# A two-block transformer layer in fp32 on one core: a weight split paced, a gate bank copied earlier, a clamp moved, filler products placed ahead of a wait

## What is computed

```python
def hybrid_layer(h, ...):                       # first layer, cut
    u = rmsnorm(h, norm_pre)
    proj = u @ w_in
    z_ssd, xbc, dt_raw, z_att, q, k, v, f_raw, g_raw = jnp.split(proj, cuts, axis=-1)
    xbc = silu(causal_depthwise_conv(xbc, conv_w, conv_b))
    y = ssd_chunked(xs_p, dt_p, a, bm_p, cm_p)  # state-space part, 4 groups x 9 chunks
    y_ssd = gated_group_rmsnorm(y + d_skip * xs, z_ssd, ssd_norm)
    y_att = forgetting_attention(qh, kh, vh, logf) * silu(z_att)
    merged = g_ssd * (y_ssd @ w_proj_ssd) + g_att * (y_att @ w_proj_att)
    return h + rmsnorm(merged @ w_out, norm_post)

def second_block(x, p, ...):                    # second layer, cut
    dq, dk, dv, bq, bk, bv, z = jnp.split(rms_norm(x) @ w_in, IN_SPLIT_IDX, axis=-1)
    dq = rms_norm(dq); dk = rms_norm(dk)        # per head, 64 wide
    a = rms_norm(diff_attention(dq, dk, dv, lam, diff_slopes))
    b = dilated_attention(rms_norm(bq), rms_norm(bk), bv, dil_slopes)
    x = x + (concat([a, b]) * silu(z)) @ w_out
    return x + sigmoid(rms_norm(x) @ w_ple_gate) * (p @ w_ple_proj)
```

## Time and profile before

| | |
|---|---|
| median of 3 executions | 2833.82 us (2832.86 to 2835.63) |
| the profiled execution | 2834.69 us, of it 2832.9 us from first to last instruction |
| PE busy | 2738.8 us, 97% of the span |
| DVE, ACT, POOL busy | 60%, 37%, 33% |
| DMA | 236.55 MB, mean 84 GB/s |
| TensorE clock granted, mean | 0.991 of full speed |

### The profile page before, as it was taken

The page is one execution under the profiler, slowest core; times in us unless marked ns, Lnnn a source line. Parts: engine busy times, 40 slices in busy tenths (PEclk is TensorE's granted clock), DMA queues, the critical chain, the costliest instruction groups (busy, mean ns, idle before and its releaser), DMA issues. The chain is left out here.

```text
span 2832.9 us, 39662 instructions
## 1 busy us (share of the span) xinstructions
PE 2738.8 (97%) x15660; PEld 2126.4 (75%) x15660; DVE 1699.7 (60%) x2674; ACT 1043.4 (37%) x1727; POOL 928.2 (33%) x549
## 2 busy tenths in 40 slices
PE   7999999999999999999999999999999999999999
PEld 6979797987778777777776887766666667776777
DVE  5787878786121345444456114776776786677586
ACT  4342524343110233333333002335666654444231
POOL 2233323232554111111111334542221134333465
PEclk8999999999999999999999999999999999999999
DMA  4131413233533111111112324531101101113643
GB/s 170 60 88 67 88 69 85 72 79 111 209 112 116 46 53 44 52 40 44 53 46 108 106 80 143 178 100 41 48 19 44 38 24 52 42 42 99 221 142 108
DMA packets 113752, 236.55 MB, mean 84 GB/s; under 512 B 9120, under 2 KB 52896, under 8 KB 113568
## 3 DMA queue, kind: packets, MB, share of 16 engines
q1 hardware_dynamic: 63312, 172.14, 18.5%
q10 hardware_dynamic: 50256, 61.87, 7.3%
HBM read 189.88 MB, written 44.11 MB: 83 GB/s over the span
## 5 line engine op out<-in xcount | busy, mean ns | idle before, releaser
L80 PE MATMUL psum<-u_h,w_hi 128*128 128x512 f32 (+2 forms) x2624 | 1011.2, 385 | 27.0 <-ACT z_gate L622 9.7
L82 PE MATMUL psum<-u_h,w_lo 128*128 128x512 f32 (+2 forms) x2624 | 963.5, 367 | 0.0
L81 PE MATMUL psum<-u_h,w_hi 128*128 128x512 f32 (+2 forms) x2624 | 962.4, 367 | 0.0
L136 POOL TENSOR_SCALAR w_hi<-w_raw 128x1024 fp32r<-128x1024 f32 x212 | 236.1, 1114 | 1418.3 <-ACTq L1368 500.3
L80 PEld LDWEIGHTS psum<-u_h,w_hi 128*128 128x128 f32 x2624 | 495.8, 189 | 158.5 <-issue 73.6
L138 POOL TENSOR_TENSOR w_lo<-w_raw,w_hi 128x1024 fp32r<-128x1024 f32 x212 | 545.2, 2572 | 17.7
L81 PEld LDWEIGHTS psum<-u_h,w_hi 128*128 128x128 f32 x2624 | 496.3, 189 | 69.6 <-issue 11.5
L82 PEld LDWEIGHTS psum<-u_h,w_lo 128*128 128x128 f32 x2624 | 495.4, 189 | 68.8
L1393 ACT ACTIVATE f_exp<-psum 128x1024 f32<-128x1024 f32 (+5 forms) x104 | 78.8, 774 | 235.0 <-PE psum L1237 128.0
L2618 ACT ACTIVATE a_exp<-a_exp 128x1024 f32<-128x1024 f32 x96 | 101.4, 1056 | 119.9 <-DVE a_exp L2790 62.5
L1487 DVE CUSTOM_DVE_ANT_0 f_junk<-psum,f_decay,f_max 128x512 f32<-128x512 f32 (+2 forms) x96 | 60.2, 664 | 103.8 <-PE psum L1260 91.1
(11 more groups left out here) (433 smaller groups left out, 4445.4 us busy)
## 6 DMA issues: line engine op xcount, KB each, us to landing
w_raw<-in_w_all SPq DMA_DIRECT2D x212, 512.0 KB, 3.5
sums_rows<-s_acs ACTq DMA_DIRECT2D x32, 512.0 KB, 8.5
f_decay<-s_nc SPq DMA_DIRECT2D x16, 520.0 KB, 5.8
s_y<-conv_out ACTq DMA_DIRECT2D x16, 512.0 KB, 2.9
yo_raw<-s_y ACTq DMA_DIRECT2D x8, 1024.0 KB, 10.9
x_tok<-in_x SPq DMA_DIRECT2D x8, 512.0 KB, 8.4
s_xT<-xT SPq DMA_DIRECT2D x8, 512.0 KB, 4.9
s_pssd<-fox_last ACTq DMA_DIRECT2D x16, 256.0 KB, 2.0
```

What stands on the lines that cost most here:

```text
L80: nc.tensor.matmul(out, w_hi[:, k], a_hi, start=(k == 0 and first), stop=False)
L81: nc.tensor.matmul(out, w_hi[:, k], a_lo, start=False, stop=False)
L82: return nc.tensor.matmul(out, w_lo[:, k], a_hi, start=False, stop=(k == kk - 1 and final))
L136: self.nc.gpsimd.tensor_scalar(self.hi[:, r], self.raw[:, r], 1.0, 1.0, ALU.mult, ALU.mult).then_inc(self.hi_done, 1)
```

## The change

Five edits. In `lead_phase`, the first weight tile's split waits between its two steps for the fifth `spread` (`split` gets an argument for it), and eight filler products stand ahead of the last `spread_rows`. In `ssd_phase`, ACT copies the gate's second bank before the exponentials of chunk 1 instead of after, and DVE's `clamp(2)` stands behind the values and b of chunk 1 instead of ahead of `decay_c(1)`. In the second block, the filler products of the item `("S", 0, GK1)` stand ahead of the wait for the small bank instead of behind it, and are 12 instead of 8.

```diff
-    def split(self, eng, i, per, n):
+    def split(self, eng, i, per, n, between=None):
...
         eng.wait_ge(self.hi_done, m + 1)
+        if between is not None:
+            eng.wait_ge(*between)
         self.nc.gpsimd.tensor_tensor(self.lo[:, r], self.raw[:, r], self.hi[:, r].bitcast(F32),
...
+            hold(nc, K, ps[:, 512 * 7:512 * 7 + P], 8)
             spread_rows(NCH - 1)
             first_projection(1, 7, range(KT))
...
-            K.W.split(pool, 0, 0, 0)
+            K.W.split(pool, 0, 0, 0, (spread, 5))
...
-                for d in (1, 2):
-                    row_exps(d)
-                    exps(d)
-                    if d == 1:
-                        zcopies(1)
+                row_exps(1)
+                zcopies(1)
+                exps(1)
+                row_exps(2)
+                exps(2)
...
                 copy_b(0)
-                clamp(2)
                 decay_c(1)
...
+                        if c == 0:
+                            clamp(2)
                         mask(c + 1)
...
                 kind, q, g = it
+                if it == ("S", 0, GK1):
+                    hold(nc, K, ps[:, MX + 512:MX + 512 + P], 12)
                 least(pe, sfree, number[it])
...
-                    if (q, g) == (0, GK1):
-                        hold(nc, K, ps[:, MX + 512:MX + 512 + P], 8)
                     pe.wait_ge(sq_ok, number_of(q, g) + 1)
```

## The result

The changed kernel takes 2840.56 us in the median of 11 runs (2836.65 to 2843.45), the kernel before 2832.86 in 11 runs beside it (2830.59 to 2837.94). The ratio is 1.0028, with an interval of 1.0020 to 1.0036: **0.28% slower**, some 7.7 us, where the forecast was 5 us faster. The profiled execution has a span of 2841.0 us against 2832.9.

What follows compares the result with a forecast made beforehand. PE was taken as the bound, busy 2738.8 of 2832.9 us. Lead phase -3.1, state-space phase +1.7 and second block -3.7 sum to -5.1 us against 2834.69, so 2828.7 us on the median's scale, range 2825.0 to 2833.0.

Steps and rivals of the forecast that it cites:

- Part 2: State-space phase: group 0 gains, groups 1 to 3 and the clock lose; a loss of 1.7 us, ends -1.5 and +6.
- the turns go to POOL: Rival, state-space phase: groups 1 to 3 lose 1.8 us each, one more clock fall; phase +5.8, time 2832.8; chance 0.17.
- The sign that I had named: Groups 1 to 3: the fourth gate product would stand behind waits of 2.5 to 3 us.
- Group 0: State-space phase: values no longer wait behind the clamp; fourth gate product at 154.4 instead of 155.69, gain 1.3 us.
- Group 2: State-space phase: POOL had got in ahead of the mask there already, so a loss of only 0.1 us.
- The copy of the gate's bank: Groups 1 to 3: exponentials behind it bring the mask 0.9 us later; it wins a small wait that `front(2)` takes back.
- The clock: Ahead of the fourth gate product idle time grows; half a 1.7 us fall for group 3, less for group 0, 1.1 together.
- The lead phase: `x_diag` stall gone, fillers free and holding the clock, SP last; next phase at 45.2 instead of 48.34, gain 3.1 us.
- The second block: 24 filler passes run before the bank is free, 3.78 us at half clock vanish; gain 3.7 us, bounds 3.0 and 4.0.
- a little: Second block: chain to the first key product keeps 7.2 us, ending 1916.95; PE finishes its own products sooner and idles a little.
- The lower bound of 3.0: Second block: gain if fillers run at half clock, 5.8 us to 1910.8, where the chain starts with the sum.
- The slower case of the prediction: Rival: two idle ends of PE per group bring five new clock falls of 1.7 us; 2839.6 us, chance 0.05.

Runs made afterwards that it cites:

- clamp_before_b: Kernel before with only the clamp of chunk 2 moved, behind the values but ahead of the copy of b; 2833.16 us, ratio 1.0001.
- ssd_only: Kernel before with the two state-space edits alone (gate's second bank copied earlier, clamp of chunk 2 later); 2837.90 us, ratio 1.0017.
- clamp_only: Kernel before with only the clamp moved behind the values and the copy of b, in all four groups; 2837.33 us, ratio 1.0016.
- zcopy_only: Kernel before with only the copy of the gate's second bank moved ahead of the exponentials of chunk 1; 2838.02 us, ratio 1.0021.
- early4: Kernel before plus four short products of ones by ones (16 columns) at PE's very start; 2832.57 us, ratio 1.0000.
- early8: Kernel before plus eight products of ones by ones (128 columns) at PE's very start; 2834.61 us, ratio 1.0012.
- early16: Kernel before plus sixteen short products of ones by ones (16 columns) at PE's very start; 2834.96 us, ratio 1.0004.
- clamp_g0: Kernel before with the clamp moved in group 0 alone, the copy of the gate's bank left where it was; 2830.39 us, ratio 0.9996.
- all_again: The changed kernel with all edits, run again beside its parts, against the kernel before; 2837.21 us, ratio 1.0021.
- all_third: The changed kernel with all edits, run once more against the kernel before; 2837.94 us, ratio 1.0019.

## Why the prediction was wrong

**The turns at the clamp: the step that failed.** Part 2 let the moved clamp start at 292.88 and end at 294.02, since in the earlier trace rows it ran undisturbed against L400 with starts 0.04 us apart. The trace after has the same 0.04 us and the other winner: 2.09 us. The rule of the Trainium skill that I weighed there and set aside ("SBUF — State Buffer", section "Who interferes with whom": of the two, the one that issues first has the port pair for the whole instruction) was the right forecast, and clamp_before_b shows it at work: with a lead of 0.16 us DVE has the turn. Read with recorded starts it still gives the wrong winner for the pair of the earlier trace rows, as I had written; what failed was to carry that pair's outcome over to another pair with the same 0.04 us. The first rival, "the turns go to POOL", had the mechanism, its price (1.8 for each group, measured 1.6, 0.7 and 1.6) and a sum for the phase of +5.8; I gave it 0.17. The steps of the phase add up to -1.3 + 3.9 + 1.6 (clock) = +4.2 in ssd_only, where I had +1.7. From 48.3 to 700.5 the five executions with the whole edit come out 4.8 us later than the kernel before's, and five with none of it 0.4 earlier: +5.2. With the turn won (clamp_before_b) groups 1 and 3 lose 0.6 each, for which 0.9 was forecast. The sign that I had named, waits of 2.5 to 3 us ahead of the fourth gate products, came true (2.7) with the wrong step behind it.

**Group 0** was right: L491 waits for `cb` (1.67 us in the changed kernel) and the fourth gate product comes 1.36 us earlier, for 1.3 forecast.

**Group 2** was counted at 0.1, since POOL had got ahead there already. It lost 0.7 in ssd_only and clamp_only: the late mask adds to that state instead of taking its place. Behind the moved copy alone it does take its place (0.0 in zcopy_only).

**The copy of the gate's bank** was right in form: ACT brings the mask later too, and the later of the two counts. zcopy_only shows that this half alone loses 1.0 us in groups 1 and 3 and nothing in group 2, and 1.6 us more by a clock that stays down for longer. What it wins is the small wait ahead of the third gate product, and the chunk loop gives it back.

**The clock** behind the state-space groups was counted at 1.1 in all. The new fall behind group 3's fourth gate product comes in each of the seven executions that move the clamp there, at 1.6 to 1.7 us (clamp_before_b's too), and in none of the ten others (among all but those of early4, early8 and early16). That term was 0.5 too small.

**The lead phase: the chain was right, the fillers were not free.** `x_diag` at 20.70 with 0.29, the next phase at 45.03, SP the last to end: each as forecast, and the 3.1 us were 3.3 in this pair of executions. But the kernel before's own execution had a long fall of the clock in this phase. The clock in stretches of 3.41 us, in the kernel before and then in clamp_g0, which has the same lead phase:

```profile
22.97:26.38 3.41, 2.50 (x10) 2.10 (x10) 3.28 (x10) 1.00 (x2) 0.11 (x1) 0.51 0.01 2
26.38:29.79 3.41, 2.33 (x7) 2.06 (x8) 3.24 (x10) 3.14 (x5) 0.00 (x0) 0.50 0.02 5
29.79:33.20 3.41, 3.41 (x16) 3.35 (x16) 2.10 (x6) 2.80 (x6) 0.00 (x0) 0.50 0.00 0
```

```profile
24.78:28.19 3.41, 1.18 (x6) 0.72 (x4) 3.24 (x12) 0.98 (x2) 0.00 (x0) 0.50 0.01 2
28.19:31.60 3.41, 2.98 (x12) 2.71 (x11) 3.24 (x12) 2.90 (x6) 0.00 (x0) 0.50 0.02 5
31.60:35.00 3.40, 3.40 (x28) 3.33 (x26) 3.00 (x10) 2.73 (x5) 0.00 (x0) 1.00 0.00 0
```

Over 17 profiled executions (all but those of early4, early8 and early16) the nine with the hold leave the phase 2.26 us earlier than that execution, the eight without it 0.48 earlier: the hold is worth 1.8 us there, where the sum had 3.1 for it and the fillers. The fillers did hold the clock as forecast: in four of the six executions with them no second fall comes in this phase, in the two others it begins at 44.9 and 47.8, as the phase ends, and in all eleven without them it begins between 38 and 41 and lasts 3.4 or 6.8 us. But costed at nothing because they fit into a gap, they cost 0.1% of the whole, about 3 us, in a part of the program that I hadn't looked at.

**The second block: priced in one unlucky execution.** 2.7 us came in this pair (1858 to 1960 in the first table), 1 less than forecast. PE no longer stands for the bank, as forecast; the key product then waits:

```profile
1925.96 0.50 PE L2375 MATMUL psum<-a_khi,a_qhi 64*128 64x512 f32 x2 [1.93 <-POOL a_klo L2252]
```

That is the idle end that the part called "a little": the chain behind the sum was to keep its 7.2 us, and takes 8.18 (ACT's L2600 at 1917.78 to the key product at 1925.96). One step in it is 1.0 us longer, DVE's second, which took 0.74 before and now meets POOL's split of the item before, `GQ0` (L2252, 1.28 us before):

```profile
1920.93 1.60 POOL L2252 TENSOR_TENSOR a_qlo<-a_un,a_qhi 128x512 fp32r<-128x512 f32 x1
...
1921.32 1.76 DVE L2805 SCALAR_TENSOR_TENSOR a_un<-a_un,a_par,a_sq 128x512 f32<-128x512 f32 x1
```

In all eight executions with this edit that step takes 1.76 us and the chain 8.18, in the twelve without it 0.74 or 0.75 and 7.2 to 7.4. A chain that begins earlier meets another engine at another point, and that is the microsecond missing here; no run takes this meeting away and keeps the rest. The lower bound of 3.0 in the prediction doesn't follow either: with fillers to 1910.8 and a sum of 0.5 us, ACT starts at 1911.3 for 1913.4, a gain of 2.1.

And the 3.78 us of filler in the earlier trace rows stood at half clock, which isn't the rule: in the eleven other executions with that code they take 2.0 to 2.5 us. ssd_only, where the code there is that of before:

```profile
1911.77 2.05 PE L156 MATMUL psum<-ones,ident 128*128 128x128 f32 x16 [2.71 <-ACT a_vT L2597]
1913.66 1.02 PE L2317 MATMUL psum<-a_sq,pairs 128*128 128x512 f32 x2
```

Between 1858 and 1960 the nine executions without the edit come out 1.36 us earlier than the kernel before's on average, the eight with it 2.50: the edit is worth 1.1 us, and 3.7 was three times that.

**The sum.** -1.8 (hold) + 3 (fillers) + 5 (state space) - 1.1 = +5, where I had -5.1. all_again, all_third and the first measurement have +5.9, +5.4 and +7.9 by their ratios. The slower case of the prediction, the only one with this outcome, counted five new falls of the clock; what came was the turns, one fall and the fillers, so its number was near and its reason was not.

## What to carry to other kernels

An instruction that is moved to where another engine starts at the same moment is priced by both orders of the two, and if the orders differ by more than the rest of the change is worth, that step decides the forecast; a place 0.2 us ahead of the other engine can then be worth more than the move itself. The same holds for a whole chain that begins earlier: look at what the other engines do at its new time. A gain that is read from one execution holds the clock's luck of that execution: compare the same stretch in a second one, or price it at both levels of the clock. And fillers that fit into a gap are still instructions: time the kernel with them alone.

## What the runs showed of the hardware

- A difference of 0.04 us between two recorded starts doesn't tell which engine has the turn at SBUF. With POOL recorded 0.03 to 0.05 us ahead, DVE had it in the earlier trace rows (POOL's L400 on 16 partitions, 2.16 us), 39 times of 39 in groups 1 to 3 of the thirteen executions with the clamp at its old place; POOL had it at the moved clamp (L403 on 128 partitions, 1.04), 18 times of 18 in six. 0.16 us ahead was enough for DVE, 3 times of 3. Why the first pair goes to DVE no run here tells.
- Eight PE products of 128 columns in an idle stretch at the program's start made the kernel 0.12% slower [0.03, 0.20]; four of 16 columns did not (1.0000), sixteen of 16 columns at most by 0.14%. The cause is open.
- Executions of one program differ by whole falls of the clock: in the lead phase a first fall of 10.2 or 6.8 us at half clock with the same code, in groups 1 and 2 a fall behind the fourth gate product or none, 1.6 us each time.
